# A fourth slab buffer for the slab behind a layer norm, and gate and up of a net's first step in one stream of 512-column matmuls

## The chip, the cores and the metric

One core of a Trainium2 chip runs the whole program. The time is the device time of one launch in microseconds (us). Before the change it is 1534.26 us, the median of 3 runs (1534.22 to 1534.91).

## The reference, cut to what matters

256 tokens of 1024 features pass through one block of a first kind and two layers of a second kind, all in f32:

```python
def first_block(...):          # once
    u = rmsnorm(h, norm_mix)
    # s5 branch and stick-breaking attention on u @ w_in, gated and merged
    h = h + merged @ w_out
    hid = relu(rmsnorm(h, norm_mlp) @ w_ff1)
    h = h + (hid * hid) @ w_ff2
    return rmsnorm(h, norm_final)

def swiglu(x, wg, wu, wd):
    return (silu(x @ wg) * (x @ wu)) @ wd

def second_block(...):         # l = 0, 1
    x = layer_norm(ALPHA*x + 0.5*swiglu(x, ffn1_wg[l], ffn1_wu[l], ffn1_wd[l]), ...)
    x = layer_norm(ALPHA*x + token_mixer(x, w_in[l], ..., w_out[l], ...), ...)
    x = layer_norm(ALPHA*x + 0.5*swiglu(x, ffn2_wg[l], ffn2_wu[l], ffn2_wd[l]), ...)
```

w_ff1 is 1024x4096, wg and wu are 1024x2816, wd is 2816x1024. There are thus five feed-forward nets: the plain one (relu squared) of the first block, called ffn1 below, and four gated ones, fa and fb of each layer l.

## The kernel before, in words

**Slabs.** Every weight is cut into slabs of 128 partitions x 2048 f32 (1 MB). A slab is loaded by SyncE (SP) into `raw` (`sp_slab`, the DMA is line 396), ScalarE (ACT) casts it to the rounded upper part `wh` (`act_round`, line 430), VectorE (DVE) subtracts to get the lower part `wl` (`dve_split`, line 437), and TensorE (PE) multiplies: each product is three matmuls, upper by upper, upper by lower, lower by upper (`mm3`, line 470; line 524 and 528 in the steps of a net, where one 512-column matmul covers upper and lower activations). `plan()` lays out one list of slabs and gives each one of three slots in turn. Four semaphores a slot order the work: SP waits for `split[slot]` before it overwrites `raw`, ACT waits for `raw_full[slot]` and for `used[slot]` of the slab before, DVE for `rounded[slot]`, PE for `split[slot]`.

**Order.** Each engine runs one order, written out by hand, and never goes past a wait. In a net `ffn_split` (lines 592 to 637) writes the same order for ACT and DVE: an opening, a loop over the steps, the last but one step, the last step. `do` is `act_round` or `dve_split` of a slab; `epilogue` is what evicts and combines the step's products. In ffn1 (16 steps of two slabs, 256 hidden features each) `step` runs first the epilogue and then `do` of the slab two places on. The numbers of slabs of ffn1 used below: 52, 54 are w_ff1 of steps 14 and 15, 53, 55, 56 are w_ff2 of steps 13, 14, 15, and 57, 58 are gate and up of the first step of net fa of layer 0. SP's order in ffn1 (`b1_sp`) is a loop that loads w_ff1 of step i and w_ff2 of step i-1, then the gains of the norm, then slab 56, then `b2_sp`: a table, and 57, 58.

**Between nets.** PE runs `rows_two` for the last two down slabs with the 128 tokens of tile 0 ahead of tile 1. For each tile DVE takes statistics (line 917) and writes the normed tile `res` (938, 947, or 944), PE transposes it (`turn_half`, line 883), ACT casts the upper part (893) and DVE subtracts the lower part (957). `big_act` rounds one slab in tile 0's part of the norm, and `big_dve` splits one slab (`next_split`) after tile 1's part.

**A gated net's start.** `first_tokens` multiplies the gate slab with the tokens as the stationary operand: tile 0 (24 matmuls of 256 columns), `turn_half` of tile 1, tile 1 (24 more). A second `first_tokens` does the up slab (48). Then step 1 begins: 8 matmuls of line 524, 8 of 528, four transposes of the first step's product (line 546), and so on. The same `first_tokens` opens the projection `in2` behind net fa, whose next slabs go through `lin_pe`.

**Other users of the buffers.** `late_prod` (8 KB a partition) is scratch of the first block's scan and of the attention; `bh`, `bl` hold split activations and the last step's hidden values.

Of the kernel before, what the change touches and what calls it, by code (L numbers as in the profile page):

```python
# [14 lines left out]
P = 128  # L15
# [15 lines left out]
WCOLS = SLAB // KD  # L31
PI = float(np.pi)
# [73 lines left out]
def plan():  # L106


    slabs, used, last = [], [0, 0, 0], [1, 2]

    def oldest():

        return 3 - sum(last)

    def add(what, part, slot=None):
        if slot is None:
            slot = oldest()
        slabs.append((what, part, slot, used[slot]))
        used[slot] += 1
        if slot != last[1]:  # L120
# [24 lines left out]
    g, s, d = oldest(), last[0], last[1]  # L145
    add("ff1", 0, g)
    for i in range(1, SLABS1):
        add("ff1", i, s)
        add("ff2", i - 1, d)
    add("ff2", SLABS1 - 1)  # L150

    def ffn(tag, l):
        g, d, u = oldest(), last[1], last[0]
        add(tag + "_g", (l, 0), g)
        add(tag + "_u", (l, 0), u)
        for i in range(1, SLABS2 - 1):
            add(tag + "_g", (l, i), g)
            add(tag + "_d", (l, i - 1), d)
            add(tag + "_u", (l, i), u)

        add(tag + "_g", (l, SLABS2 - 1), g)
        add(tag + "_u", (l, SLABS2 - 1), u)
        add(tag + "_d", (l, SLABS2 - 2), d)
        add(tag + "_d", (l, SLABS2 - 1))

    for l in range(LAYERS):
        mark(("fa", l))
        ffn("fa", l)
        mark(("in2", l))
        for n in (6, 0, 1, 2, 3, 4, 5):  # L170
            add("in2", (l, n))
        mark(("uq", l))
        add("uq", (l, 0))
        mark(("ukv", l))
        add("ukv", (l, 0))
        mark(("gate2", l))
        for n in range(8):
            add("gate2", (l, n))
        mark(("proj", l))
        for n, w in enumerate(("proj_m", "proj_n", "proj_m", "proj_n")):  # L180
            add(w, (l, n // 2))
        mark(("out2", l))
        for n in range(4):
            add("out2", (l, n))
        mark(("fb", l))
        ffn("fb", l)
    return slabs, where


def hybrid_ssm_attention_kernel(nc, a, out):  # L190
# [9 lines left out]
    loads_so_far, total = [], [0, 0, 0]  # L200
# [4 lines left out]
    with ExitStack() as ctx:  # L205
# [9 lines left out]
        raw = sb("raw", [P, 3, SLAB])  # L215
        wh = sb("wh", [P, 3, SLAB], F32R)
        wl = sb("wl", [P, 3, SLAB], F32R)
# [5 lines left out]
        bh = sb("bh", [P, KD, T], F32R)  # L223
        bl = sb("bl", [P, KD, T], F32R)
# [9 lines left out]
        late_prod = sb("late_prod", [P, 2, 4, T])  # L234
# [29 lines left out]
        raw_full = [sem(f"raw_full{i}") for i in range(3)]  # L264
        rounded = [sem(f"rounded{i}") for i in range(3)]
        split = [sem(f"split{i}") for i in range(3)]
        used = [sem(f"used{i}") for i in range(3)]
# [247 lines left out]
        def ffn_pe(pe, n0, iters, has_up, ih0, j):  # L515
# [70 lines left out]
            if has_up:  # L586
# [3 lines left out]
                     lambda: last_hidden(n1 + per, iters - 1, bh, bl))  # L590

        def ffn_split(eng, do, n0, iters, has_up, epilogue, opening, then=None):
# [29 lines left out]
            if last + 3 < len(slabs):  # L622
# [35 lines left out]
        def ffn_act_engine(act, n0, iters, has_up, ih0, j, scale):  # L658
            net = net_index(j)

            def epilogue(what, n, i, more, between=None):
# [23 lines left out]
                b = 6 if isinstance(i, int) and i == 1 and not has_up else 4  # L685
# [7 lines left out]
            def first_step(n, function, s):  # L693
                wait_used(act, n)
                act.activation(act_out[:, :, :], two(bank[4]), function).then_inc(s, 1)
# [5 lines left out]
            def opening_gated():  # L701
                act_round(act, n0 + 3)
                first_step(n0, ACT.Silu, ffn_act)
                act_round(act, n0 + 2)
                seed(act, j, 0, scale, 0)
                act_round(act, n0 + 4)
                round_product(7)
                epilogue("gate", n0 + 2, 1, 0)
                seed(act, j, 0, scale, 1)
                silu("gate", 1)  # L710
                act_round(act, n0 + 5)
                epilogue("up", n0 + 4, 1, 0)
                act_round(act, n0 + 6)

            def opening_plain():
                act_round(act, n0 + 2)
                first_step(n0, ACT.Relu, relu_done)
# [8 lines left out]
        def ffn_dve_engine(dve, n0, iters, has_up, ih0, j):  # L726
            net = net_index(j)

            def epilogue(what, n, i, more, between=None):

                if what == "gate" and not has_up and isinstance(i, int) and i == iters - 1:
                    link = lambda ins: chain(dve, dve_n, dve_chain, ins)
                    for f in range(2):
# [18 lines left out]
                        ins = dve.tensor_copy(bh[:, f, :], hid[:, f, :])  # L752
# [5 lines left out]
                        ins = dve.tensor_tensor(bl[:, f, :], hid[:, f, :], bh[:, f, :].bitcast(F32), ALU.subtract)  # L758
                    ins.then_inc(hid_ready, 1)
                    return  # L760
                if what == "gate":
                    dve.wait_ge(gate_half, i + (ih0 - net))
                    b = 6 if isinstance(i, int) and i == 1 and not has_up else 4
# [9 lines left out]
                if has_up and isinstance(i, int) and i == iters - 1:  # L773
# [5 lines left out]
                    link(dve.tensor_copy(bh[:, 0, :], hid[:, 0, :]))  # L779
                    dve.tensor_tensor(bl[:, 0, :], hid[:, 0, :], bh[:, 0, :].bitcast(F32), ALU.subtract)  # L780
# [24 lines left out]
                xh, xl = (bh[:, 0:2, :], bl[:, 0:2, :]) if last else (hh[:, :, :], hl[:, :, :])  # L805
# [265 lines left out]
        prod += [late_prod[:, i, :, :] for i in range(2)]  # L1071
# [42 lines left out]
        def first_tokens(pe, n, b, j=None):  # L1114
# [12 lines left out]
            mm.then_inc(used[slot], 1)  # L1127

# [51 lines left out]
        def b1_sp(sp):  # L1180
# [596 lines left out]
        def b1_act(act):  # L1777
# [121 lines left out]
            big_act(act, 2, N_FFN1 + 2 * SLABS1 + 1, 1)  # L1899

        def b1_dve(dve):
# [86 lines left out]
            big_dve(dve, 2, True, N_FFN1 + 2 * SLABS1 + 1)  # L1988
# [24 lines left out]
        late = late_prod[:, :, :, :].rearrange("p i a t -> p (i a t)")  # L2013
# [5 lines left out]
        cmp_w1 = [t_.rearrange("p (s c) -> p s c", s=16) for t_ in (late_prod[:, :, :, :].rearrange("p i a t -> p (i a t)"),  # L2019
# [33 lines left out]
        def b2_ffn_sp(sp, l, tag):  # L2053
            n0 = where[(tag, l)]
            sp_slab(sp, n0)
# [7 lines left out]
            gain_loads(sp, j)  # L2063
            for n in range(3 * SLABS2 - 4, 3 * SLABS2):
                sp_slab(sp, n0 + n)

        def b2_sp(sp, l):
# [4 lines left out]
            for n in range(where[("in2", l)], where[("fb", l)]):  # L2072
                if n == where[("in2", l)] + 4:
                    for i, nm in enumerate(("cmp_k_w1_2", "cmp_v_w1_2")):
# [276 lines left out]
        def b2_act(act, l):  # L2351
# [3 lines left out]
            big_act(act, nj, where[("in2", l)] + 1, 3)  # L2355
            n0 = where[("in2", l)]
            act_round(act, n0 + 2)
            wait_used(act, n0)
            act.copy(vsw, bank[5].rearrange("p (a w d) -> p a w d", a=NTT, w=2)).then_inc(v_read, 1)
            for i in range(6):  # L2360
                n = n0 + 1 + i
                act_round(act, n + 2)
# [83 lines left out]
            for q in range(3):  # L2446
                act_round(act, where[("out2", l)] + q + 2)
            big_act(act, nj + 1, where[("out2", l)] + 5, 3)
            ffn_act_engine(act, where[("fb", l)], SLABS2, True, SLABS1 + (2 * l + 1) * SLABS2, nj + 2, 2 * ALPHA)
            if l < LAYERS - 1:  # L2450
                big_act(act, nj + 2, where[("fb", l)] + 3 * SLABS2 + 1, 3)
# [42 lines left out]
        def b2_dve(dve, l):  # L2494
# [5 lines left out]
            big_dve(dve, nj, False, n0 + 1)  # L2500
            dve_split(dve, n0 + 2)
# [99 lines left out]
            for q in range(4):  # L2601
                if q < 3:
                    dve_split(dve, where[("out2", l)] + q + 2)
            big_dve(dve, nj + 1, False, where[("out2", l)] + 5)
            ffn_dve_engine(dve, where[("fb", l)], SLABS2, True, SLABS1 + (2 * l + 1) * SLABS2, nj + 2)
            if l < LAYERS - 1:
                big_dve(dve, nj + 2, False, where[("fb", l)] + 3 * SLABS2 + 1)
# [89 lines left out]
```

## Time and profile before

| | |
|---|---|
| profiled execution | 1534.03 us, of which the span is 1532.3 us |
| PE busy | 1504.0 us (98%), 9541 matmuls |
| DVE busy | 1059.5 us (69%) |
| ACT busy | 809.3 us (53%) |
| line 437, DVE (split) | x238, 513.7 us, mean 2170 ns |
| line 430, ACT (round) | x238, 429.0 us, mean 1812 ns |
| DMA | 265.08 MB, 173 GB/s |
| granted clock of TensorE | 0.999 |

PE is busy all but 28 us, so a step of another engine counts only where PE waits for it. A matmul's busy time (392 ns with 512 columns) is longer than the distance to the next one, since they are pipelined; distances are read from start to start.

### The profile page before, as it was taken

The numbers are of one execution on the slowest core, as the hardware profiler recorded it, in microseconds if no ns is written. First come the engines' busy times: TensorE is split into PE (matmuls) and PEld (weight loads), VectorE is DVE, ScalarE is ACT, GpSimd is POOL, SyncE is SP. The second block draws the span as 40 slices with busy tenths as digits, with TensorE's granted clock in tenths as the row PEclk, the third lists the DMA queues.
The fourth block names the chain that finished last, engine by engine and source line by source line (L and its number), as shares of the span: only waits on it lengthen the run. The fifth ranks groups of instructions, "written<-read, shape, count | busy, mean of one in ns | idle before, by whom it ended". The sixth has DMA issues, their size and how long they took to land.

```text
span 1532.3 us, 24066 instructions
## 1 busy us (share of the span) xinstructions
PE 1504.0 (98%) x9541; PEld 1321.5 (86%) x9541; DVE 1059.5 (69%) x1371; ACT 809.3 (53%) x1066; POOL 20.8 (1%) x50
## 2 busy tenths in 40 slices
PE   8999999999999999999999999999999999999998
PEld 7988988888888889898988888888889888888887
DVE  7999776667565666876766557665676866765666
ACT  7877653334444445666454444544445765454443
POOL 1011000000000000000000000000000000000000
PEclk9999999999999999999999999999999999999999
DMA  9432546556555666434455565465574524546653
GB/s 259 134 103 91 191 137 196 182 196 241 192 192 192 211 191 173 138 111 138 156 174 197 187 219 189 141 219 189 194 227 137 175 80 131 186 152 206 205 178 109
DMA packets 207021, 265.08 MB, mean 173 GB/s; under 512 B 14186, under 2 KB 176356, under 8 KB 206948
## 3 DMA queue, kind: packets, MB, share of 16 engines
q1 hardware_dynamic: 206884, 264.04, 53.6%
q8 instruction: 51, 0.84, 0.2%
q14 instruction: 22, 0.18, 0.0%
q10 hardware_dynamic: 64, 0.02, 0.0%
HBM read 262.99 MB, written 1.05 MB: 172 GB/s over the span
## 4 chain that ended last, share of the span: by engine, by line
PE 91%; DVE 6%; ACT 1%; DMA 0%; issue 0%; SPq 0%; DVEq 0%; ACTq 0%
PE bank L470 48%; PE bank L524 23%; PE bank L528 12%; DVE wl L437 2%; PE bank L2110 2%; PE bank L2124 1%; PE bank L1462 1%; PE bank L2139 1%; DVE u_parts L957 1%; ACT wh L430 1%; PE bank L1449 1%; DVE res L947 0%; DMA raw<-w_in 0%; DVE sq L938 0%; ACT u_parts L893 0%; PE bank L2114 0%
## 5 line engine op out<-in xcount | busy, mean ns | idle before, releaser
L437 DVE TENSOR_TENSOR wl<-raw,wh 128x2048 fp32r<-128x2048 f32 (+4 forms) x238 | 513.7, 2170 | 181.1 <-ACT wh L430 179.2
L430 ACT CAST wh<-raw 128x2048 fp32r<-128x2048 f32 (+4 forms) x238 | 429.0, 1812 | 121.8 <-PE bank L470 117.7
L524 PE MATMUL bank<-u_parts,wh 128*128 128x512 f32 x1520 | 380.0, 392 | 0.1
L524 PEld LDWEIGHTS bank<-u_parts,wh 128*128 128x128 f32 x1520 | 276.5, 189 | 52.3 <-issue 0.8
L470 PE MATMUL bank<-u_parts,wh 128*128 128x256 f32 (+1 forms) x1344 | 252.2, 289 | 7.0 <-DVE wl L437 4.5
L528 PEld LDWEIGHTS bank<-u_parts,wl 128*128 128x128 f32 x1520 | 207.4, 190 | 14.8
L470 PEld LDWEIGHTS bank<-u_parts,wh 128*128 128x128 f32 (+1 forms) x1344 | 208.1, 190 | 12.7 <-issue 7.0
L528 PE MATMUL bank<-u_parts,wl 128*128 128x256 f32 x1520 | 211.9, 282 | 0.0
L470 PE MATMUL bank<-u_parts,wl 128*128 128x256 f32 (+1 forms) x672 | 189.8, 282 | 0.0
L470 PE MATMUL bank<-wh,hh 128*128 128x512 f32 x440 | 172.3, 392 | 0.5
L470 PE MATMUL bank<-wl,hh 128*128 128x512 f32 x440 | 171.9, 391 | 0.0
L470 PE MATMUL bank<-wh,hl 128*128 128x512 f32 x440 | 171.3, 389 | 0.0
L470 PE MATMUL bank<-wh,u_parts 128*128 128x256 f32 (+1 forms) x608 | 139.1, 319 | 3.4 <-DVE u_parts L957 1.9
L470 PEld LDWEIGHTS bank<-u_parts,wl 128*128 128x128 f32 (+1 forms) x672 | 127.9, 190 | 0.0
L686 ACT COPY gates<-bank 128x512 f32<-128x512 f32 x54 | 31.6, 586 | 160.7 <-PE bank L528 160.7
L470 PEld LDWEIGHTS bank<-wh,u_parts 128*128 128x128 f32 x608 | 102.1, 190 | 13.9 <-DVE u_parts L957 3.4
L681 ACT COPY gates<-bank 128x512 f32<-128x512 f32 x36 | 21.1, 586 | 158.5 <-PE bank L528 158.5
L470 PEld LDWEIGHTS bank<-wh,hl 128*128 128x128 f32 x440 | 82.7, 188 | 17.6
L470 PEld LDWEIGHTS bank<-wh,hh 128*128 128x128 f32 x440 | 82.8, 188 | 16.8 <-issue 1.2
L470 PE MATMUL bank<-wl,u_parts 128*128 128x256 f32 (+1 forms) x304 | 96.3, 317 | 0.0
L470 PEld LDWEIGHTS bank<-wl,hh 128*128 128x128 f32 x440 | 82.8, 188 | 15.1
L792 DVE TENSOR_TENSOR gates<-gates,bank 128x512 f32<-128x512 f32 x36 | 24.8, 688 | 97.0 <-ACT gates L681 97.0
(371 smaller groups left out, 1780.7 us busy)
## 6 DMA issues: line engine op xcount, KB each, us to landing
raw<-ffn_wg SPq DMA_DIRECT2D x44, 1024.0 KB, 5.4
raw<-ffn_wu SPq DMA_DIRECT2D x44, 1024.0 KB, 5.3
raw<-ffn_wd SPq DMA_DIRECT2D x44, 1024.0 KB, 5.1
raw<-w_ff SPq DMA_DIRECT2D x32, 1024.0 KB, 5.3
raw<-w_in SPq DMA_DIRECT2D x28, 1024.0 KB, 6.1
raw<-w_out SPq DMA_DIRECT2D x12, 1024.0 KB, 4.9
raw<-w_gate SPq DMA_DIRECT2D x8, 1024.0 KB, 5.5
raw<-w_in SPq DMA_DIRECT2D x16, 512.0 KB, 5.3
```

The costliest lines, as they stand in the source:

```text
L430: ins = act.copy(dst, src)
L437: ins = dve.tensor_tensor(dst, src, upper.bitcast(F32), ALU.subtract)
L470: mm = pe.matmul(o, w, x, start=start and n == 0, stop=stop and n == 2, skip_group_check=True)
L524: return pe.matmul(two(bank[b + f]), slab_view(wh, slot, KD, WCOLS)[:, k, f * P:(f + 1) * P], u_parts[:, k, :, :], start=k == 0, stop=Fals ...
L528: return pe.matmul(bank[b + f][:, 0:T], slab_view(wl, slot, KD, WCOLS)[:, k, f * P:(f + 1) * P], uh[:, k, :], start=False, stop=k == KD - ...
L681: act.copy(up_z, halves(6)[1]).then_inc(up_half_out, 1)
L686: act.copy(gate_z, halves(b)[1]).then_inc(gate_half, 1)
L792: dve.tensor_tensor(up_z, up_z, halves(6)[0], ALU.add).then_inc(up_sum, 1)
L957: dve.tensor_tensor(ul[:, k, c], bank[2 * tt + half].rearrange("p (k t) -> p k t", k=4), uh[:, k, c].bitcast(F32), ALU.subtract).then_inc( ...
L1449: mm = pe.matmul(bank[s % 2][:, part * T:(part + 1) * T], b_t[part][r, i, :], us[r, i, :], start=True, stop=True, skip_group_check=True)
L1462: mm = pe.matmul(bank[3][32 * j:32 * j + 32, 0:T], c_t[c][:, s, :], prod[s % 4][:, q, :], start=n == 0, stop=n == 3)
L2110: pe.matmul(bank[e][:, c], q_(slice(tt * P, (tt + 1) * P)), k_(slice(0, (tt + 1) * P)), start=tt == 0, stop=True, skip_group_check=True)
```

## The change

A fourth slot, `LEAD` = 3, is added to `raw`, `wh`, `wl`. It takes the gate slab of each gated net's first step and the first slab of `in2`. To make room, `late_prod` becomes `raw[LEAD]`, and `bh`, `bl` become `wh[LEAD]`, `wl[LEAD]`; the last step's hidden values get small tiles `lasth`, `lastl`. The lead slab is rounded and split before the last but one step of the net ahead of it, and the slab behind it moves up by one place everywhere: what was split after the norm was the second slab, and is now the third.

```diff
-        bh = sb("bh", [P, KD, T], F32R)
-        bl = sb("bl", [P, KD, T], F32R)
+        bh, bl = (w[:, LEAD, :].rearrange("p (k t) -> p k t", k=KD) for w in (wh, wl))
+        lasth = sb("lasth", [P, 2, T], F32R)
+        lastl = sb("lastl", [P, 2, T], F32R)
...
@@ ffn_pe
-            first_tokens(pe, n0, 4, j - 1)
+            if has_up:
+                pair_tokens(pe, n0, 4, j - 1)
+            else:
+                first_tokens(pe, n0, 4, j - 1)
             n1 = n0 + (2 if has_up else 1)
-            if has_up:
-                first_tokens(pe, n0 + 1, 6)
-                pe.wait_ge(ffn_act, ih0 - SLABS1 + 1)
-                gate(n1, turn=7)
-            else:
+            if not has_up:
                 pe.wait_ge(res_copy_act, 4)
-                gate(n1, b=6, turn=5)
+            gate(n1, b=6, turn=4 if has_up else 5)
             down(n1 + 1, 0)
             if has_up:
+                pe.wait_ge(gate_sum, ih0 - net + 1)
                 up_half(n1 + 2, 0, 6)
...
@@ ffn_split (ACT and DVE)
             with eng.Fori(2, iters - 2, 1) as i:
                 turn(i, i - 1, n1)
+            last = n1 + per * (iters - 2)
+            lead = last + per + 1
+            if lead < len(slabs):
+                do(eng, lead)
             turn(iters - 2, 0, n1 + per * (iters - 3))
-            last = n1 + per * (iters - 2)
...
+            if has_up:
                 do(eng, last + 3)
+            else:
+                do(eng, lead + 1)
...
-                if last + 4 < len(slabs):
-                    do(eng, last + 4)
+                if lead + 1 < len(slabs):
+                    do(eng, lead + 1)
...
@@ opening_gated (ACT)
                 act_round(act, n0 + 3)
-                first_step(n0, ACT.Silu, ffn_act)
-                act_round(act, n0 + 2)
+                first_step(n0, halves(4)[1], ACT.Silu, ffn_act)
...
@@ opening_gated (DVE)
                 dve_split(dve, n0 + 3)
-                dve_split(dve, n0 + 2)
-                wait_used(dve, n0 + 1)
                 dve.wait_ge(ffn_act, ih0 - SLABS1 + 1)
-                dve.tensor_tensor(hid[:, :, :], act_out[:, :, :], two(bank[6]), ALU.mult).then_inc(hid_step, 1)
-                lower_product(7)
+                dve.tensor_tensor(hid[:, :, :], act_out[:, :, :], halves(4)[0], ALU.mult).then_inc(hid_step, 1)
+                lower_product(4)
...
+        def pair_tokens(pe, n, b, j):
+            slot = pe_slab(pe, n + 1)
+            pe_slab(pe, n)
+            both = lambda buf, k: buf[:, slot:LEAD + 1:LEAD - slot, k * WCOLS:(k + 1) * WCOLS]
+            for tt in range(NTT):
+                c = slice(tt * P, (tt + 1) * P)
+                if tt == 1:
+                    turn_half(pe, j, 1)
+                for k in range(KD):
+                    if k % 4 == 0:
+                        pe.wait_ge(norm_out, parts_count(j, tt, k // 4))
+                    if tt + 1 < NTT or k + 1 < KD:
+                        mm3(pe, two(bank[b + tt]), uh[:, k, c], ul[:, k, c], both(wh, k), both(wl, k), k == 0, k == KD - 1)
+                ... # tile 1, k = 7: six matmuls of 256 columns, so that each slot has its own release
...
@@ b1_sp
             with sp.Fori(1, SLABS1, 1) as i:
                 sp_slab(sp, n0 + 1, i, i - 1)
                 sp_slab(sp, n0 + 2, i - 1, i - 1)
+            sp.wait_ge(y_done, ST)
+            sp_slab(sp, where[("fa", 0)])
             sp.wait_ge(tok_out, out_count(BIG["mlp1"], 1, 1))
             gain_loads(sp, BIG["final1"])
...
@@ b2_ffn_sp
             gain_loads(sp, j)
+            if n0 + 3 * SLABS2 < len(slabs):
+                sp_slab(sp, n0 + 3 * SLABS2)
             for n in range(3 * SLABS2 - 4, 3 * SLABS2):
...
@@ b2_sp
+                if n == where[("out2", l)] + 1:
+                    sp.wait_ge(o_done, NU * (l + 1))
+                    sp_slab(sp, where[("fb", l)])
...
@@ ACT and DVE behind out2 (both alike)
-            for q in range(3):
-                act_round(act, where[("out2", l)] + q + 2)
-            big_act(act, nj + 1, where[("out2", l)] + 5, 3)
+            n = where[("out2", l)]
+            act_round(act, n + 2)
+            act_round(act, where[("fb", l)])
+            act_round(act, n + 3)
+            act_round(act, where[("fb", l)] + 1)
+            big_act(act, nj + 1, where[("fb", l)] + 2, 3)
```

## Rows read from the trace of the kernel before

**Rows 1.** The page's chain that ended last: share of the span by engine.

```profile
PE 91%; DVE 6%; ACT 1%; DMA 0%; issue 0%; SPq 0%; DVEq 0%; ACTq 0%
```

**Rows 2.** Busy time by stretch, two net openings: start:end, length, busy (count), clock, DMA.

```profile
769.50:784.20 14.70, 13.41 (x107) 12.58 (x106) 12.33 (x13) 7.96 (x9) 0.00 (x0) 1.00 0.24 76
389.80:403.50 13.70, 12.93 (x106) 12.48 (x106) 11.03 (x12) 7.96 (x9) 0.00 (x0) 1.00 0.27 83
```

**Rows 3.** Timeline of PE, opening of fa, layer 1: start, duration, line, [idle before].

```profile
962.20 0.66 PE L883 MATMUL bank<-ident,res 128*128 128x128 f32 x4 [0.80 <-DVE res L947]
...
966.45 0.39 PE L470 MATMUL bank<-wh,u_parts 128*128 128x256 f32 x1 [0.50 <-DVE wl L437]
```

**Rows 4.** Chain of waits in order of time: start, us; 512 columns, then 256.

```profile
354.34 5.47 PE bank L470 x24
...
611.53 5.75 PE bank L470 x48
```

**Rows 5.** Timeline of PE, opening of fa, layer 0.

```profile
392.75 1.23 PE L883 MATMUL bank<-ident,res 128*128 128x128 f32 x8
394.75 0.39 PE L470 MATMUL bank<-wh,u_parts 128*128 128x256 f32 x1 [0.77 <-DVE u_parts L957]
```

**Rows 6.** Timeline of PE, second slab of in2, layer 0.

```profile
585.76 0.50 PE L470 MATMUL bank<-u_parts,wh 128*128 128x256 f32 x2 [0.51 <-DVE wl L437]
```

**Rows 7.** Timeline of SP, end of ffn1: the loads' issues.

```profile
364.28 0.37 SPq L396 DMA_DIRECT2D raw<-w_ff  x1
364.86 0.35 SPq L985 DMA_DIRECT2D tmp<-norm_final  x1
```

**Rows 8.** Timeline of DVE, end of ffn1.

```profile
361.80 2.29 DVE L437 TENSOR_TENSOR wl<-raw,wh 128x2048 fp32r<-128x2048 f32 x1
366.02 0.69 DVE L764 TENSOR_TENSOR gates<-gates,bank 128x512 f32<-128x512 f32 x1 [1.94 <-ACT gates L686]
367.84 2.29 DVE L437 TENSOR_TENSOR wl<-raw,wh 128x2048 fp32r<-128x2048 f32 x1 [1.12 <-ACT wh L430]
```

**Rows 9.** Timeline of ACT, end of ffn1.

```profile
365.41 0.59 ACT L686 COPY gates<-bank 128x512 f32<-128x512 f32 x1 [3.64 <-PE bank L528]
365.89 1.92 ACT L430 CAST wh<-raw 128x2048 fp32r<-128x2048 f32 x1
...
373.69 0.37 ACT L674 COPY gates<-bank 128x256 f32<-128x256 f32 x1 [0.85 <-PE bank L528]
```

**Rows 10.** Timeline of PE, end of ffn1: last step's first matmul, last slab's first.

```profile
370.68 0.39 PE L524 MATMUL bank<-u_parts,wh 128*128 128x512 f32 x1
...
380.68 0.47 PE L470 MATMUL bank<-wh,bh 128*128 128x512 f32 x1 [1.53 <-DVE bl L758]
```

**Rows 11.** DMA issues at 542.92 and 543.35: count, KB, us to landing.

```profile
raw<-ffn_wu SPq DMA_DIRECT2D x1, 1024.0 KB, 5.3
...
raw<-ffn_wd SPq DMA_DIRECT2D x1, 1024.0 KB, 7.4
```

**Rows 12.** Timeline of PE, start of the program: matmuls on zeros.

```profile
4.86 3.57 PE L1004 MATMUL bank<-zero_w 128*128 128x256 f32 x15 [4.86 <-POOL cvalid L1230]
...
11.12 1.43 PE L1004 MATMUL bank<-zero_w 128*128 128x256 f32 x10
```

**Rows 13.** Busy time by stretch, end of the program; clock third from last.

```profile
1525.00:1526.00 1.00, 0.87 (x4) 0.38 (x2) 0.34 (x2) 0.00 (x0) 0.00 (x0) 1.00 1.01 375
1530.00:1531.00 1.00, 0.00 (x0) 0.00 (x0) 0.00 (x0) 0.00 (x0) 0.00 (x0) 0.85 1.00 375
```

**Rows 14.** Timelines of SP, ACT and DVE, end of fa, layer 0.

```profile
527.35 0.42 SPq L989 DMA_DIRECT2D tmp<-ln_f_b  x1
...
537.86 1.92 ACT L430 CAST wh<-raw 128x2048 fp32r<-128x2048 f32 x1
...
546.76 2.29 DVE L437 TENSOR_TENSOR wl<-raw,wh 128x2048 fp32r<-128x2048 f32 x1 [2.49 <-ACT wh L430]
```

**Rows 15.** Timeline of DVE, out2, layer 0: slabs 113 and 114.

```profile
752.22 4.65 DVE L437 TENSOR_TENSOR wl<-raw,wh 128x2048 fp32r<-128x2048 f32 x2 [1.11 <-ACT wh L430]
```

More of the change, by code:

```diff
@@ L31 @@
 WCOLS = SLAB // KD
+LEAD = 3
 PI = float(np.pi)
@@ L106, in plan @@
 def plan():
-    slabs, used, last = [], [0, 0, 0], [1, 2]
+    slabs, used, last = [], [0, 0, 0, 0], [1, 2]
     def oldest():
@@ L119, in add @@
         used[slot] += 1
-        if slot != last[1]:
+        if slot != LEAD and slot != last[1]:
             last[:] = [last[1], slot]
@@ L152, in ffn @@
     def ffn(tag, l):
-        g, d, u = oldest(), last[1], last[0]
-        add(tag + "_g", (l, 0), g)
+        g, d, u = last[0], last[1], oldest()
+        add(tag + "_g", (l, 0), LEAD)
         add(tag + "_u", (l, 0), u)
@@ L170, in plan @@
         for n in (6, 0, 1, 2, 3, 4, 5):
-            add("in2", (l, n))
+            add("in2", (l, n), LEAD if n == 6 else None)
         mark(("uq", l))
@@ L214, in hybrid_ssm_attention_kernel @@
         bank = [banks[:, i, :] for i in range(8)]
-        raw = sb("raw", [P, 3, SLAB])
-        wh = sb("wh", [P, 3, SLAB], F32R)
-        wl = sb("wl", [P, 3, SLAB], F32R)
+        raw = sb("raw", [P, 4, SLAB])
+        wh = sb("wh", [P, 4, SLAB], F32R)
+        wl = sb("wl", [P, 4, SLAB], F32R)
         res = sb("res", [P, KD, T])
@@ L261, in hybrid_ssm_attention_kernel @@
         affine = norm_small[:, 28:32].rearrange("p (a s) -> p a s", a=NTT)
[L264 to L267, printed above, removed]
+        raw_full = [sem(f"raw_full{i}") for i in range(4)]
+        rounded = [sem(f"rounded{i}") for i in range(4)]
+        split = [sem(f"split{i}") for i in range(4)]
+        used = [sem(f"used{i}") for i in range(4)]
         dve_chain, act_chain, pool_chain = sem("dve_chain"), sem("act_chain"), sem("pool_chain")
@@ L684, in epilogue @@
                     act.wait_ge(hid_ready, i + ih0)
-                b = 6 if isinstance(i, int) and i == 1 and not has_up else 4
+                b = 6 if isinstance(i, int) and i == 1 else 4
                 act.copy(gate_z, halves(b)[1]).then_inc(gate_half, 1)
@@ L691, in silu, with first_step @@
                     act.activation(act_out[:, :, :], gate_z, ACT.Silu).then_inc(ffn_act, 1)
-            def first_step(n, function, s):
+            def first_step(n, z, function, s):
                 wait_used(act, n)
-                act.activation(act_out[:, :, :], two(bank[4]), function).then_inc(s, 1)
+                act.activation(act_out[:, :, :], z, function).then_inc(s, 1)
             def round_product(b):
@@ L716, in opening_plain @@
                 act_round(act, n0 + 2)
-                first_step(n0, ACT.Relu, relu_done)
+                first_step(n0, two(bank[4]), ACT.Relu, relu_done)
                 for tt in range(NTT):
@@ L757, in epilogue @@
                             link(ins)
-                        ins = dve.tensor_tensor(bl[:, f, :], hid[:, f, :], bh[:, f, :].bitcast(F32), ALU.subtract)
+                        ins = dve.tensor_tensor(lastl[:, f, :], hid[:, f, :], lasth[:, f, :].bitcast(F32), ALU.subtract)
                     ins.then_inc(hid_ready, 1)
@@ L762, in epilogue @@
                     dve.wait_ge(gate_half, i + (ih0 - net))
-                    b = 6 if isinstance(i, int) and i == 1 and not has_up else 4
+                    b = 6 if isinstance(i, int) and i == 1 else 4
                     dve.tensor_tensor(gate_z, gate_z, halves(b)[0], ALU.add).then_inc(gate_sum, 1)
@@ L778, in epilogue @@
                     link(dve.tensor_tensor(hid[:, 0, :], act_out[:, 0, :], up_z[:, 0, :], ALU.mult))
-                    link(dve.tensor_copy(bh[:, 0, :], hid[:, 0, :]))
-                    dve.tensor_tensor(bl[:, 0, :], hid[:, 0, :], bh[:, 0, :].bitcast(F32), ALU.subtract)
+                    link(dve.tensor_copy(lasth[:, 0, :], hid[:, 0, :]))
+                    dve.tensor_tensor(lastl[:, 0, :], hid[:, 0, :], lasth[:, 0, :].bitcast(F32), ALU.subtract)
                     dve.wait_ge(up_half_out, i + (ih0 - SLABS1 + 1 - net))
@@ L804, in epilogue @@
                 last = isinstance(i, int) and i == iters - 1
-                xh, xl = (bh[:, 0:2, :], bl[:, 0:2, :]) if last else (hh[:, :, :], hl[:, :, :])
+                xh, xl = (lasth[:, :, :], lastl[:, :, :]) if last else (hh[:, :, :], hl[:, :, :])
                 dve.tensor_copy(xh, hid[:, :, :]).then_inc(hid_step, 1)
@@ L1070, in hybrid_ssm_attention_kernel @@
         prod = [small[:, i * 1024:(i + 1) * 1024].rearrange("p (a t) -> p a t", a=4) for i in range(2)]
-        prod += [late_prod[:, i, :, :] for i in range(2)]
+        prod += [raw[:, LEAD, i * 1024:(i + 1) * 1024].rearrange("p (a t) -> p a t", a=4) for i in range(2)]
         ATT = 3 * P
@@ L1127, in first_tokens @@
             mm.then_inc(used[slot], 1)
+        def pair_tokens(pe, n, b, j):
[11 more added lines that the diff above has]
+                        mm3(pe, two(bank[b + tt]), uh[:, k, c], ul[:, k, c], both(wh, k), both(wl, k), k == 0, k == KD - 1)
+                for x, w in ((uh, wl), (ul, wh), (uh, wh)) if tt == NTT - 1 else ():
+                    for i, s in enumerate((slot, LEAD)):
+                        mm = pe.matmul(two(bank[b + tt])[:, i, :], x[:, KD - 1, c], w[:, s, (KD - 1) * WCOLS:KD * WCOLS],
+                                       start=False, stop=True, skip_group_check=True)
+                        if x is uh and w is wh:
+                            mm.then_inc(used[s], 1)
         def lin_quarter(pe, n, b, j):
@@ L2012, in hybrid_ssm_attention_kernel @@
         ctok = [small[:, 512 + P * i:512 + P * (i + 1)] for i in range(2)]
-        late = late_prod[:, :, :, :].rearrange("p i a t -> p (i a t)")
+        late = raw[:, LEAD, :]
         probs = [flat(hid)[:, 0:ATT], flat(act_out)[:, 0:ATT], late[:, 0:ATT], late[:, ATT:2 * ATT]]
@@ L2018, in hybrid_ssm_attention_kernel @@
         x_f = [flat(t_).rearrange("p (s c) -> p s c", s=16) for t_ in (act_out, hid)]
-        cmp_w1 = [t_.rearrange("p (s c) -> p s c", s=16) for t_ in (late_prod[:, :, :, :].rearrange("p i a t -> p (i a t)"),
+        cmp_w1 = [t_.rearrange("p (s c) -> p s c", s=16) for t_ in (late,
                                                                     gflat[:, 2048:4096])]
@@ L2071, in b2_sp @@
             b2_ffn_sp(sp, l, "fa")
-            for n in range(where[("in2", l)], where[("fb", l)]):
+            for n in range(where[("in2", l)] + 1, where[("fb", l)]):
                 if n == where[("in2", l)] + 4:
+                    sp.wait_ge(split[LEAD], slabs[where[("in2", l)]][3] + 1)
                     for i, nm in enumerate(("cmp_k_w1_2", "cmp_v_w1_2")):
@@ L2354, in b2_act @@
             ffn_act_engine(act, where[("fa", l)], SLABS2, True, SLABS1 + 2 * l * SLABS2, nj, 2 * ALPHA)
-            big_act(act, nj, where[("in2", l)] + 1, 3)
+            big_act(act, nj, where[("in2", l)] + 2, 3)
             n0 = where[("in2", l)]
-            act_round(act, n0 + 2)
+            act_round(act, n0 + 3)
             wait_used(act, n0)
@@ L2600, in b2_dve @@
                 dve_up(dve, where[("proj", l)], l + 1, q)
[L2601 to L2604, printed above, removed]
+            n = where[("out2", l)]
+            dve_split(dve, n + 2)
+            dve_split(dve, where[("fb", l)])
+            dve_split(dve, n + 3)
+            dve_split(dve, where[("fb", l)] + 1)
+            big_dve(dve, nj + 1, False, where[("fb", l)] + 2)
             ffn_dve_engine(dve, where[("fb", l)], SLABS2, True, SLABS1 + (2 * l + 1) * SLABS2, nj + 2)
             if l < LAYERS - 1:
-                big_dve(dve, nj + 2, False, where[("fb", l)] + 3 * SLABS2 + 1)
+                big_dve(dve, nj + 2, False, where[("fb", l)] + 3 * SLABS2 + 2)
         J_LAST = 8
```

27 lines of the change are left out of this document (12 added, 15 removed).

## The prediction

> **What bounds the kernel now.** I read the chain of waits first. By engine, 91% of the span is TensorE and 6% VectorE [rows 1], so time is saved only where TensorE waits, or by making its stream shorter, and lost wherever something new makes it wait. The busy times by stretch say where it waits: the opening behind a norm. From the first product of tile 0 to the first matmul of step 1 it takes 14.6 us, in which TensorE is busy 13.4 [rows 2] (the first row, fb of layer 0; fa and fb of layer 1 have the same stretch to 0.1 us, so there are three openings of this kind). Behind ffn1 it takes 13.6 us (the second row there). The timeline of TensorE in that stretch names the waits: transposes that wait for DVE's normed tile, and the second slab, which waits 0.50 us for the split that stands behind the norm on DVE [rows 3]. The second slab of in2 waits 0.51 us for the same split [rows 6], once in each layer.
>
> **The opening, from 96 narrow products to a pair.** The chain of waits gives 24 matmuls of 512 columns 5.47 us, 228 ns each, and 48 of 256 columns 5.75 us, 119.8 ns each [rows 4]. The new opening is tile 0 of both slabs, 24 x 0.228 = 5.47; the eight transposes with the cast and the subtract behind them, 2.00 us from their start to the next product [rows 5] (392.75 to 394.75); tile 1, 21 x 0.228 + 6 x 0.120 = 5.51. Together 12.98. Tile 0 now lasts longer than DVE's work on tile 1: before, the last normed half let the transposes go at 962.20 [rows 3], 4.5 us after tile 0's first product at 957.7, against 5.47; so the wait for `res` is gone, and what is late next is the cast and subtract within the 2.00. Both slabs are split before the norm, so the wait of 0.50 is gone too. The gain is 14.6 - 13.0 = 1.6 us in three openings and 13.6 - 13.0 = 0.6 behind ffn1, 5.4 us in all. Of each, 45 x (2 x 119.8 - 228) ns = 0.5 us comes from wider matmuls, the rest from waits. The bounds: if the wide ones gave nothing and the transposes waited as before, the four gains would be near 2 us in all; the upper bound is the 2.00 shrunk by at most another 0.7 us each (the wait of 0.77 in it [rows 5]), 8 us.
>
> The Trainium skill has a formula that speaks against this part: "TensorE: Matmul & The Clock Gate", section "Back-to-back issue gap", gives the isolated distance as N/2.4 + 2.5 ns, so one wide matmul would save 2.5 ns against two narrow ones. By it the pairs would give 0.1 us a net and not 0.5, and the time below would be 1.6 us higher. The trace does not agree: 2 x 119.8 - 228 is 12 ns [rows 4].
>
> **What follows the pair.** Silu and the product with up now start when the pair ends. In the rows' durations that is some 1.5 us (one ACT and one DVE pass of 512 columns, 0.6 and 0.69, with their handovers), and the transposes of the product come 2.8 us after the pair: cost 0. Step 1's slab is split by then (DVE ends it some 2.3 us behind the norm, with 5.5 us of tile 1 to cover it). The added wait for `gate_sum` ahead of up stands behind a whole down slab, 5.47 us [rows 4], that hides a copy, a split and a sum (0.6 + 2.3 + 0.7): cost 0.
>
> **in2.** Its first slab is the lead, its second is split before the norm: the wait of 0.51 goes [rows 6], twice, 1.0 us. Bounds 0 and 1.0.
>
> **The lead's rounding and splitting in the nets fa and fb.** One more ACT pass of 1.9 and DVE pass of 2.3 us stand ahead of step 9. In fa of layer 0 ACT would do it at 537.86 [rows 14] and push the two works behind it; DVE has 2.49 us idle ahead of the next split [rows 14] (at 546.76), and that split is wanted by TensorE only at 554. The load is issued behind the gains, at some 527.8 [rows 14], and lands near 537.2 (about 3.1 MB ahead of and with it at some 370 GB/s, from 528): it is there 0.7 us before ACT asks. Cost 0; up to 1 us in each of three nets if it lands 3 us later. In out2 the split goes between slabs 113 and 114: DVE's two in a row start at 752.22 and take 4.65 us [rows 15]; with the lead between them slab 114 is ready at 759.1, and TensorE wants it at 760.8. Cost 0, in both layers.
>
> **The lead in ffn1: here the change adds a wait that nothing hides.** `ffn_split` puts the lead after step 13. SP's loop runs to the last step, so it issues slab 55 only when DVE has split 53, which is 361.80 + 2.29 [rows 8], the load goes out at 364.28 [rows 7], and the lead's load behind it at some 364.7. But ACT has rounded 53 by then, and its next instruction is the rounding of the lead. Two 1 MB loads issued 0.43 us apart landed 5.3 and 7.4 us after their issues [rows 11]; so the lead lands at 364.7 + 7.4 = 372.1. Behind the waiting ACT stand the eviction of step 14 (now at 365.41) and the rounding of 54 (365.89) [rows 9]; behind the waiting DVE the sum (0.69) and the split of 54 (2.29) [rows 8]. From there: ACT rounds the lead to 374.1, evicts and rounds 54 to 376.5; DVE splits the lead 374.2 to 376.4, sums to 377.0, splits 54 to 379.3. TensorE wanted 54 at 370.68 [rows 10]. It has nothing else in its order, and is still for 8.6 us. The bounds are 6.5 (the lead landing 5.3 us after its issue, as a lone load does) and 9.6 (the gains and slab 56 sharing the engines with it).
>
> The later part of ffn1 moves with it: from 370.68 to the last slab's first product it was 10.0 us, of which 1.53 waiting [rows 10], set by DVE from the eviction at 373.69 [rows 9] on; that chain had 0.9 us of slack ahead, since DVE was splitting.
>
> **The clock after such a stop.** At the end of the program TensorE is idle from 1525.9, the granted clock is 1.00 at first and falls within 1530 to 1531 [rows 13], 4 to 5 us later. A stop of 8.6 us is longer, so it will fall from 2.4 to 1.2 GHz. At the program's start 15 matmuls of 256 columns took 3.57 us and ten later ones 1.43 [rows 12], so coming back costs 3.57 - 15 x 0.12 = 1.8 us of work. It lies in front of the eviction that sets the chain; less the slack of 0.9 it is 0.9 us. If the first half of the step (2.8 us of work) all ran at half the clock, it is 1.9. I take 1.2; the lower bound is -0.1, no fall.
>
> The Trainium skill has this as a rule, in "TensorE: Matmul & The Clock Gate", Part 1: an idle array goes to half its clock and returns only after sustained work. By that rule, the trace agrees [rows 12, 13]; without it the sum would be 1.3 us lower, the first rival below.
>
> **The sum.** 1534.03 (the profiled execution; its span 1532.3 and 1.7 around it) + 8.6 + 1.2 - 5.4 - 1.0 = 1537.4. The median of the runs lies 0.2 above that execution; I say 1537.5. The rest of the change (scratch moved into slot 3, small tiles) moves no instruction.
>
> **The rivals.** 0.2% is 3.1 us, about what a measurement of this kernel tells from no change: 1531.2 to 1537.3 is "same".
>
> *The clock holds* (or returns at once): 1536.2. For it: the end of the program is the one place where the trace shows it falling. Against it: the stop is twice as long as what it took there. Not slower. It decides from 0.3 us of the 1.2 on, so it is near the forecast.
>
> *The wait in ffn1 is hidden*, with all the gains left: 1534.3 - 6.4 = 1527.9. The point from which it decides: each us that the lead lands earlier is one us less; to be faster by 0.2% it must land near 366.8 or before. Against it, the issue at 364.28 of the load ahead of it [rows 7] and 5.3 us for even a lone load.
>
> *The openings give little*: TensorE reads two slots' halves in one matmul slower than one row of them, or the transposes, now behind the whole pair of tile 0, are what tile 1 waits for, or a lead in fa or fb lands late. Gains of 2 in place of 6.4: 1542.
>
> **How the numbers follow.** The forecast (stall, fallen clock, gains as counted) 0.47, with its own range 1536.5 to 1539.5; clock holds 0.27; openings give little 0.13; stall hidden or short 0.13. Slower by over 0.2%: two thirds of the forecast's cases, the openings' case and a few of the second, 0.50; same 0.37; faster 0.13. The range 1533.8 to 1541.5 leaves out the hidden stall and half of the openings' case.
>
> **What would show it.** A gap of TensorE of 8 to 9 us ahead of ffn1's last step, with ACT's rounding of `ffn_wg` waiting some 10 us for a DMA before it, and the granted clock at half behind it. Openings of 13.0 us with matmuls of 512 columns 228 ns apart. No wait at in2's second slab, and no new gap between steps 8 and 10 of fa and fb or in out2. I am wrong if the gap is not there: then the lead's load went out before slab 55's, or ACT was not behind it.

## The result and the profile after

The changed kernel takes 1537.64 us, median of 12 runs (1537.15 to 1538.39); the kernel before, on the same chip, 1534.25 (12 runs, 1533.90 to 1534.91). The ratio is 1.0023, 95% interval 1.0015 to 1.0031: slower by 3.4 us, and the 1537.64 is 0.14 above the forecast of 1537.5. The profiled execution of after took 1537.29 with a span of 1535.5.

The shares of the chain by engine, the row that answers to [rows 1]:

```profile
PE 93%; DVE 5%; ACT 1%; DMA 1%; issue 0%; SPq 0%; DVEq 0%; ACTq 0%
```

TensorE has gone from 91 to 93% and VectorE from 6 to 5%: the waits behind the norms are shorter. DMA's share, rounded, is 1% where it was 0: the chain of both kernels has one load at the program's start (7.41 us before, 6.26 after), and that of after has a second one of 7.38 us, at the end of ffn1. The issues on SP there, against [rows 7]; then ACT, DVE and TensorE, against [rows 8, 9, 10] (start, duration, engine, line, operation, count, and the idle time before it with what ended it):

```profile
359.25 5.38 SPq L397 DMA_DIRECT2D raw<-w_ff  x2
364.84 0.38 SPq L397 DMA_DIRECT2D raw<-ffn_wg  x1
```

```profile
359.82 1.92 ACT L431 CAST wh<-raw 128x2048 fp32r<-128x2048 f32 x1 [3.07 <-PE bank L471]
372.25 1.90 ACT L431 CAST wh<-raw 128x2048 fp32r<-128x2048 f32 x1 [10.51 <-DMA raw<-ffn_wg]
374.05 0.58 ACT L692 COPY gates<-bank 128x512 f32<-128x512 f32 x1
374.53 3.70 ACT L431 CAST wh<-raw 128x2048 fp32r<-128x2048 f32 x2
384.39 0.37 ACT L680 COPY gates<-bank 128x256 f32<-128x256 f32 x1 [6.16 <-PE bank L529]
```

```profile
374.18 2.29 DVE L438 TENSOR_TENSOR wl<-raw,wh 128x2048 fp32r<-128x2048 f32 x1 [10.11 <-ACT wh L431]
376.39 0.68 DVE L769 TENSOR_TENSOR gates<-gates,bank 128x512 f32<-128x512 f32 x1
376.99 2.28 DVE L438 TENSOR_TENSOR wl<-raw,wh 128x2048 fp32r<-128x2048 f32 x1
380.98 2.28 DVE L438 TENSOR_TENSOR wl<-raw,wh 128x2048 fp32r<-128x2048 f32 x1
```

```profile
379.42 3.75 PE L525 MATMUL bank<-u_parts,wh 128*128 128x512 f32 x8 [8.61 <-DVE wl L438]
...
384.13 1.99 PE L525 MATMUL bank<-u_parts,wh 128*128 128x512 f32 x8
...
390.62 0.47 PE L471 MATMUL bank<-wh,lasth 128*128 128x512 f32 x1 [0.80 <-DVE lastl L763]
```

Read them from the top. SP issues the load of the lead (`ffn_wg`) at 364.84, behind slab 55's. ACT has been waiting for it since 361.74 and rounds it at 372.25. The copy for step 14, which it did at 365.41 before [rows 9], stands behind that and runs at 374.05; then come two roundings in a row, of slabs 54 and 55. DVE waits 10.11 us for the lead, splits it, sums, and splits slab 54 by 379.27. TensorE stands still for 8.61 us ahead of the last step. The idle time that the costliest group of TensorE's lines gives as ended by a split is this one stop:

```profile
L525 PE MATMUL bank<-u_parts,wh 128*128 128x512 f32 x1520 | 381.8, 394 | 8.7 <-DVE wl L438 8.6
```

The granted clock around it, in windows of 1 us (start:end, length, busy and count of PE, PEld, DVE, ACT and POOL, then the clock, the DMA share and GB/s):

```profile
372.00:373.00 1.00, 0.00 (x0) 0.00 (x0) 0.00 (x0) 0.75 (x1) 0.00 (x0) 1.00 1.01 401
373.00:374.00 1.00, 0.00 (x0) 0.00 (x0) 0.00 (x0) 1.00 (x1) 0.00 (x0) 0.60 1.04 418
374.00:375.00 1.00, 0.00 (x0) 0.00 (x0) 0.82 (x1) 1.00 (x3) 0.00 (x0) 0.50 1.01 406
...
382.00:383.00 1.00, 1.00 (x4) 0.71 (x4) 1.00 (x1) 0.00 (x0) 0.00 (x0) 0.50 1.08 385
383.00:384.00 1.00, 1.00 (x8) 1.00 (x7) 0.26 (x1) 0.00 (x0) 0.00 (x0) 0.78 0.87 301
384.00:385.00 1.00, 1.00 (x7) 0.87 (x6) 0.21 (x1) 0.61 (x2) 0.00 (x0) 1.00 0.26 54
```

It falls to half (1.2 GHz) early between 373 and 374, some 2.4 us into the stop (TensorE is idle from 370.81), and comes back in the middle between 383 and 384, some 4 us after TensorE resumed at 379.42. The eight matmuls of 512 columns at 379.42 take 3.75 us, the next eight of the same kind, at 384.13, take 1.99.

An opening, fa of layer 1, against [rows 2, 3] (timeline of TensorE):

```profile
964.77 0.39 PE L471 MATMUL bank<-wh,u_parts 128*128 128x512 f32 x1
...
970.22 1.04 PE L886 MATMUL bank<-ident,res 128*128 128x128 f32 x8
972.22 0.51 PE L471 MATMUL bank<-wh,u_parts 128*128 128x512 f32 x1 [0.96 <-DVE u_parts L960]
972.56 0.40 PE L471 MATMUL bank<-wl,u_parts 128*128 128x512 f32 x1
...
977.87 1.32 PE L525 MATMUL bank<-u_parts,wh 128*128 128x512 f32 x5
```

Tile 0 takes 5.45 us, the eight transposes run at once (no idle time ahead of them), the next product is 2.00 behind their start, tile 1 takes 5.65. Together 13.10. And the second slab of in2, layer 0, against [rows 6]: its first matmul is 0.12 us behind the last of the first slab, with no wait.

```profile
594.27 0.28 PE L471 MATMUL bank<-wh,u_parts 128*128 128x256 f32 x1
594.39 0.40 PE L471 MATMUL bank<-u_parts,wh 128*128 128x256 f32 x2
594.63 0.28 PE L471 MATMUL bank<-u_parts,wl 128*128 128x256 f32 x1
```

I laid the two traces beside each other at matching matmuls: after is 9.94 us late at ffn1's last slab (390.62 against 380.68 [rows 10]). From there it gains 0.57 in fa's opening of layer 0, 0.81 in in2, 1.50 in fb's, then 1.51, 0.84 and 1.50 in layer 1: 6.73 in all, and the end is 3.21 late. Between these places the offset stays within 0.03 us, so nothing else in fa, fb or out2 moved the end. All this is the profiled execution. The cost of the stop is not the same in every run: seven of the twelve took 1537.15 to 1537.72 us with a mean clock of 0.996 to 0.997, five took 1538.06 to 1538.39 with 0.995 to 0.996.

### The profile page after: what moved, and what is told of

Same layout as the page of the kernel before. It is cut to its first block, busy times and chain, and to the rows that moved or that the text cites. A ratio compares the mean times of both kernels' runs of the same rounds, so it can differ in the third digit from the quotient of the medians.

```text
span 1535.5 us, 23711 instructions
## 1 busy us (share of the span) xinstructions
PE 1500.9 (98%) x9361; PEld 1313.3 (86%) x9361; DVE 1058.2 (69%) x1371; ACT 807.8 (53%) x1066; POOL 20.7 (1%) x50
## 4 chain that ended last, share of the span: by engine, by line
PE 93%; DVE 5%; ACT 1%; DMA 1%; issue 0%; SPq 0%; DVEq 0%; ACTq 0%
PE bank L471 49%; PE bank L525 23%; PE bank L529 12%; PE bank L2141 2%; DVE wl L438 1%; PE bank L2155 1%; PE bank L1488 1%; PE bank L2170 1%; ACT wh L431 1%; PE bank L1475 1%; DMA raw<-ffn_wg 0%; DVE u_parts L960 0%; PE bank L2145 0%; PE bank L886 0%; DMA small<-log_dt 0%; PE bank L2131 0%
## 5 line engine op out<-in xcount | busy, mean ns | idle before, releaser
L471 PE MATMUL bank<-wh,u_parts 128*128 128x512 f32 (+1 forms) x472 | 129.3, 356 | 5.0 <-DVE u_parts L960 5.0
L471 PEld LDWEIGHTS bank<-wh,u_parts 128*128 128x128 f32 x472 | 84.1, 189 | 19.4 <-DVE u_parts L960 6.6
L471 PE MATMUL bank<-wl,u_parts 128*128 128x512 f32 (+1 forms) x236 | 83.5, 354 | 0.0
```

The lines of the kernel that those rows point to most:

```text
L471: mm = pe.matmul(o, w, x, start=start and n == 0, stop=stop and n == 2, skip_group_check=True)
```

## The experiments

Is it the place of the lead's load that costs, and is it the whole of the loss? In e1_early_load SP issues it one step earlier, ahead of the last step's two slabs, and the rest stays:

```diff
-            with sp.Fori(1, SLABS1, 1) as i:
+            with sp.Fori(1, SLABS1 - 1, 1) as i:
                 sp_slab(sp, n0 + 1, i, i - 1)
                 sp_slab(sp, n0 + 2, i - 1, i - 1)
             sp.wait_ge(y_done, ST)
             sp_slab(sp, where[("fa", 0)])
+            sp_slab(sp, n0 + 2 * SLABS1 - 3)
+            sp_slab(sp, n0 + 2 * SLABS1 - 2)
```

> The changed kernel with one thing moved: SP issues the lead's load of ffn1 ahead of the loads of the last step's slabs, one step (11 us) earlier; ACT's and DVE's order is unchanged. My theory (ACT and DVE waited for that load, and TensorE for them): the gap of 8.6 us ahead of ffn1's last step and the half clock behind it are gone, TensorE's first product of the last slab comes 10.0 us after the last step's first matmul as before, and all gains stay: 1537.6 - 9.9 = 1527.7 us. Rival 1, the extra rounding and splitting itself delays TensorE in ffn1: a gap of some 2.3 us stays there, 1530. Rival 2, the fallen clock was the main cost: 1536.4.

Measured 1527.68 us (5 runs, 1527.57 to 1527.72), ratio to before 0.9957 (0.9944 to 0.9971). The load now goes out at 353.83 and lands 7.6 us later, some 0.3 us before ACT asks for it. Its timeline and TensorE's:

```profile
359.85 3.73 ACT L431 CAST wh<-raw 128x2048 fp32r<-128x2048 f32 x2 [3.07 <-PE bank L471]
365.41 0.59 ACT L692 COPY gates<-bank 128x512 f32<-128x512 f32 x1 [1.83 <-PE bank L529]
```

```profile
370.67 1.98 PE L525 MATMUL bank<-u_parts,wh 128*128 128x512 f32 x8
...
380.68 0.47 PE L471 MATMUL bank<-wh,lasth 128*128 128x512 f32 x1 [1.53 <-DVE lastl L763]
```

The lead's rounding (the second of the two at 359.85) fits where ACT idled, the copy is at 365.41 as before, and the last step and the last slab stand where they stood [rows 10]. So the stop and its clock cost the 9.9 us between 1537.64 and 1527.68 (each against its own runs of before), and the openings with in2 are worth 6.5. Both rivals fall: no gap of 2.3 us is left, and far more than the clock's part has come back.

Does the position in ACT's and DVE's order cost, or the position of the load? In e2_round_later the load stays late, and the plain net rounds and splits the lead one step later:

```diff
-            if lead < len(slabs):
+            if has_up and lead < len(slabs):
                 do(eng, lead)
             turn(iters - 2, 0, n1 + per * (iters - 3))
+            if not has_up:
+                do(eng, lead)
```

> The changed kernel with ffn1's lead rounded and split behind the last but one step instead of ahead of it; its load is where it was. My theory: the load has landed by then (372.1), the gap ahead of the last step is gone, but the split (2.3 us) now stands ahead of DVE's chain for the last slab, which TensorE awaits: 1527.7 + 2.2 = 1529.9 us. Rival (only the place of the load counts, whoever waits for it): 1537.6.

Measured 1531.28 (11 runs, 1529.66 to 1532.55), ratio 0.9982 (0.9973 to 0.9991): 1.4 above what was expected. The stop of 8.6 us is gone, but a smaller one stands ahead of the last slab, and in it the clock falls (timeline, then windows):

```profile
383.06 0.76 PE L471 MATMUL bank<-wh,lasth 128*128 128x512 f32 x1 [3.74 <-DVE lastl L765]
```

```profile
382.00:383.00 1.00, 0.00 (x0) 0.00 (x0) 0.89 (x4) 1.00 (x2) 0.00 (x0) 0.81 1.10 347
383.00:384.00 1.00, 0.94 (x2) 0.83 (x3) 1.00 (x1) 0.02 (x1) 0.00 (x0) 0.50 1.06 340
385.00:386.00 1.00, 1.00 (x4) 0.81 (x3) 0.24 (x1) 0.00 (x0) 0.00 (x0) 0.50 0.96 385
386.00:387.00 1.00, 1.00 (x5) 0.82 (x5) 0.70 (x1) 0.00 (x0) 0.00 (x0) 0.98 0.59 71
```

Three microseconds at half are 1.5 us of work, and the last slab is 2.2 us later than in the kernel with the early load (383.06 against 380.68, less 0.17, by which this execution is already late at the ACT rounding: 360.02 against 359.85). 1527.7 + 2.2 + 1.5 = 1531.4. The expectation had the wait and not the clock. The runs bear that out: one of the eleven took 1529.66 with a mean clock of 0.999, close to the 1529.9 expected without a fall; seven took 1531.12 to 1531.41 with 0.998, and three 1532.08 to 1532.55 with 0.997. So behind the same stop a run lost nothing, some 1.6 or some 2.6 us, and its mean clock goes along; only one of those with 0.998 has a trace. Either edit takes the long stop away; only the earlier load takes all of it.

How much does the clock cost? In e5_keep_clock sixty matmuls on zeros into a free bank keep TensorE busy in the stop:

```diff
             n1 += per * (iters - 2)
+            if not has_up:
+                keep_clock(pe, 60, 6)
             gate(n1, 0, iters - 1, by_tile=not has_up)
```

> The changed kernel with 60 matmuls of 256 columns on zeros into an unused bank ahead of ffn1's last step (7.2 us of work, inside the gap of 8.6). My theory of the clock's part: the granted clock stays at 2.4 GHz, and the last slab's first product follows the last step's first matmul by 9.9 us, not 11.2: 1537.6 - 1.3 = 1536.3 us. Rival (the 1.2 us came from the order of splits, not from the clock): 1537.6.

Measured 1535.77 (11 runs, 1535.60 to 1536.13), ratio 1.0011 (1.0002 to 1.0020). Timeline of TensorE, to be held against the two rows of after:

```profile
370.69 7.35 PE L1009 MATMUL bank<-zero_w 128*128 128x256 f32 x60
379.60 2.08 PE L525 MATMUL bank<-u_parts,wh 128*128 128x512 f32 x8 [1.56 <-DVE wl L438]
```

The wait for the data ends at nearly the same time (379.60 for 379.42), but the eight matmuls take 2.08 us, not 3.75, and the clock stays at 1.00. From the step's first matmul to the last slab's it is 9.36 us here (to 388.96) and 11.20 in after. The clock costs 1.84 us in this pair of executions, and the medians, 1.87 apart, say the same. Expected were 1.3: the rival (the order of splits, not the clock) falls, and the price was taken 0.5 too small.

How much do the 512-column matmuls give, and how much the order? Two kernels with the early load. In the first, e3_narrow, each wide matmul is two of 256 columns, and the order stays:

```diff
-                        mm3(pe, two(bank[b + tt]), uh[:, k, c], ul[:, k, c], both(wh, k), both(wl, k), k == 0, k == KD - 1)
+                    for i, s in enumerate((slot, LEAD)) if tt + 1 < NTT or k + 1 < KD else ():
+                        q = slice(k * WCOLS, (k + 1) * WCOLS)
+                        mm3(pe, two(bank[b + tt])[:, i, :], uh[:, k, c], ul[:, k, c], wh[:, s, q], wl[:, s, q],
+                            k + i == 0, k == KD - 1)
```

> e1_early_load with the pair's matmuls cut into two of 256 columns in the same order (96 in place of 51 matmuls a net). What the wide ones are worth by the rows of before, 45 x 12 ns in each of four nets: 2.1 us, so 1529.8 us. Rival, 2.5 ns each: 1528.2. If the two-slot operand made the wide ones slower than one row of 512, it would be under 1527.7.

Measured 1529.55 (6 runs, 1529.34 to 1529.70), ratio 0.9969 (0.9957 to 0.9981): 1.87 us above the wide one, over 4 openings of 45 wide matmuls each, so 10.4 ns for each. That is near the forecast's 12 [rows 4]. From the isolated distance, N/2.4 + 2.5 ns, in the Trainium skill's "TensorE: Matmul & The Clock Gate", section "Back-to-back issue gap", the estimate is 2.5 ns for each, 0.45 us in all; the two medians differ by four times that.

In the second, e4_slab_order, the slabs come one after the other, as before the change, and only the early split is left:

```diff
-            for tt in range(NTT):
-                c = slice(tt * P, (tt + 1) * P)
-                if tt == 1:
-                    turn_half(pe, j, 1)
+            for i, s in ((1, LEAD), (0, slot)):
+                for tt in range(NTT):
+                    c = slice(tt * P, (tt + 1) * P)
+                    if tt == 1 and i == 1:
+                        turn_half(pe, j, 1)
...
-                first_step(n0, halves(4)[1], ACT.Silu, ffn_act)
+                first_step(n0 + 1, halves(4)[1], ACT.Silu, ffn_act)
```

> e3_narrow (1529.55 us) with the order of the opening turned back: the lead slab's two tiles first, then the second slab's two tiles, 96 matmuls of 256 columns; the slabs are still both split ahead of the norm, and silu waits for the second slab. So the transposes of tile 1 wait for DVE's normed tile again. My theory: tile 1 begins 5.06 us after tile 0 as in the kernel before, then 72 x 0.12 us follow, 13.8 against 13.5 us, in three openings +0.3, behind ffn1 +0.1: 1530.6 us. Rival: the new order is what the openings gained from, then it is near the old 14.6 us, 1532.5.

Measured 1530.28 (9 runs, 1530.06 to 1531.01), ratio 0.9975 (0.9965 to 0.9985). The transposes of tile 1 in the opening of fa, layer 1, and the product behind them:

```profile
959.85 0.66 PE L886 MATMUL bank<-ident,res 128*128 128x128 f32 x4
961.29 0.66 PE L886 MATMUL bank<-ident,res 128*128 128x128 f32 x4 [0.79 <-DVE res L950]
961.90 0.39 PE L471 MATMUL bank<-wh,u_parts 128*128 128x256 f32 x1
```

The wait for `res` [rows 3] is back, but from the first transpose to the product it is 2.05 us, and in after, where the wait is gone, 2.00: there the product waits 0.96 for the cast and subtract instead. So the pair's order is worth little, 1530.28 - 1529.55 = 0.73 us, 0.18 an opening. The 3.8 us that this kernel is ahead of its own runs of before (1534.12) belong to the early splits: 1.65 in in2 (the two offsets above) and some 2.2 in the openings. The trace agrees: this opening takes 13.83 us (956.82 to 970.65) and took 14.57 (957.74 to 972.31), 0.74 less, and there are three of its kind.

The openings still hold the 0.96 us ahead of tile 1 and the transposes themselves. The last kernel, e6_early_turn, with the early load and the wide pair, puts the transposes of tile 1 into tile 0's stream, the first half ahead of block 6 and the second at its end:

```diff
-                if tt == 1:
-                    turn_half(pe, j, 1)
                 for k in range(KD):
...
+                    if tt == 0 and k == 6:
+                        turn_part(pe, j, 1, 0)
...
+                if tt == 0:
+                    turn_part(pe, j, 1, 1)
```

> e1_early_load (1527.68 us) with tile 1's transposes moved into tile 0's matmuls: half 0 after the sixth k, half 1 at the end of tile 0, in the four gated openings. In the changed kernel TensorE has an idle 1.1 of the 2.0 us from the transposes to tile 1's first product. My theory: the normed half is there 3 us after tile 0's start, the transposes at 4.1 us make tile 1 ready at 6.1, and tile 0 with its transposes ends at 6.4, so the idle goes in all four: 1527.7 - 4.4 = 1523.3 us. Rival: the normed halves are late, or what follows the pair (silu, product, transposes) becomes the wait: 1525 to 1527.7.

Measured 1522.85 (5 runs, 1522.75 to 1523.07), ratio 0.9926 (0.9913 to 0.9940). It is faster than both kernels. The same opening, by its end and in one window from its first product to step 1:

```profile
956.85 0.60 PE L891 MATMUL bank<-ident,res 128*128 128x128 f32 x4
...
958.68 0.60 PE L891 MATMUL bank<-ident,res 128*128 128x128 f32 x4
959.03 0.48 PE L471 MATMUL bank<-wh,u_parts 128*128 128x512 f32 x1
```

```profile
952.74:964.62 11.88, 11.88 (x61) 9.95 (x60) 9.61 (x12) 4.56 (x5) 0.00 (x0) 1.00 0.03 8
```

TensorE is busy in all of the 11.88 us; with the early load alone the stretch was 13.09 (954.98 to 968.07). Four times 1.2 is the 4.8 between 1527.68 and 1522.85. The transposes come in two groups of four with the last six matmuls of tile 0 between them, so the first cast and subtract have those to cover them, and the second have the first four blocks of tile 1.

## Why the prediction was right, step by step

**The stop in ffn1: right in place, cause and size.** 8.6 us were predicted, and 8.61 of idle time measured (8.7 from the step's old start to its new one: 370.68 to 379.42). Every link of the chain came within 0.2 us: landing 372.1 and measured 372.2; the lead rounded at 374.1 and 374.15; split of 54 ending at 379.3 and 379.27. The choice of 7.4 us from issue to landing [rows 11], not the 5.3 of a lone load, made it: the load took 7.38 here. The early load took the stop away and put the end at 1527.68, where the forecast had 1527.9 for a hidden wait.

**The clock: right that it falls; the sum met by luck, with two errors of opposite sign.** 1.2 us were taken for the clock after the slack; the kernel with zeros shows 1.84 on the chain, of some 2.0 us of work lost in 4 us at half. The slack of 0.9 was not where it was put: it is in the warm chain, which got shorter by 0.64 us (9.36 against 10.00), where I had 0.1. The cause is in ACT's rows: 54 and 55 were rounded in one go at 374.53, so DVE no longer waited for the rounding of 55 and split it 1.56 us behind the step's first matmul (380.98 - 379.42, and the same in the kernel with zeros); before it was 2.20 (372.88 - 370.68). In both warm kernels DVE's sum for the step's first eviction stands directly behind that split (375.09 and 383.37), so the 0.64 between the two is what the chain got shorter. So the sum 1.84 - 0.64 = 1.2 met the 1.2 taken by luck, by two terms each 0.5 to 0.6 off. The first rival (the clock holds) fell. The Trainium skill says in "TensorE: Matmul & The Clock Gate", Part 1, that an idle array goes to half its clock and comes back only after sustained work; the windows of after agree (0.50 at 374, after 3.2 us idle, and 1.00 again some 4 us behind the first matmul).

**The openings: right.** 13.10 us for 12.98 predicted in fa of layer 1; the remainder is tile 1, 5.65 for 5.51, whose first matmul behind the wait is 0.34 us ahead of the second (972.22 to 972.56) where 0.228 was counted. The gains were 0.57, 1.50, 1.51 and 1.50, together 5.1 for 5.4. What was late next was the cast and subtract, as said, at 2.00. What the step did not say is that the wait for `res`, which went, gave almost nothing, since the cast and subtract took its place; the gain is the split's wait (0.74 in the kernel with slabs one after the other) and the wider matmuls (1.87 over four openings, 0.47 each); with the 0.18 of the order that is 1.4 of the 1.5. Of the rival (the openings give little) nothing is left: a matmul that reads two slots' halves has the distance of 0.23 of one that reads a row.

**in2: the mechanism right, the term too small.** 0.5 a layer was counted from the idle column [rows 6], and 0.81 and 0.84 were gained. That column runs from a matmul's modelled end, 0.28 us behind its start, while starts without a wait are 0.12 apart. 0.16 is missing from each wait that is read that way, so 0.51 was 0.67. Another 0.10 is the first matmul behind the wait: in before the third stands 0.34 us behind it (585.76 to 586.10, below), in after 0.24 (594.39 to 594.63). The last 0.04 to 0.07 is open.

```profile
586.10 0.28 PE L470 MATMUL bank<-u_parts,wl 128*128 128x256 f32 x1
```

**The edits costed at nothing: right.** The offset does not move between the openings, so the leads in fa and fb, the split in out2 and the wait for `gate_sum` were hidden. The lead in fa of layer 0 was nearer to a wait than the 0.7 us said (and 3.1 MB at 370 GB/s from 528 is 536.4, not the 537.2 written): in the kernel with narrow matmuls ACT waits 0.26 us for that load (`w_in`), which TensorE does not feel.

```profile
538.33 3.72 ACT L431 CAST wh<-raw 128x2048 fp32r<-128x2048 f32 x2 [0.26 <-DMA raw<-w_in]
```

**The sum.** 8.7 + 1.84 - 0.64 - 6.73 = +3.2, by the spans 1535.5 - 1532.3 = 3.2, for +3.4 forecast (8.6 + 1.2 - 6.4). The misses in the gains, 0.3 less than forecast in the openings and 0.65 more in in2, have opposite signs too, and both are smaller than the spread of the runs.

## What to carry to other kernels

When an instruction is moved forward in the order of an engine that works in order, move the load that feeds it forward in its queue too, and look up when it lands; everything written behind it waits with it, even what is ready. Here a change that gave 6.5 us cost 9.9 by the place of one load. Add to a stop of TensorE what the clock costs behind it (here 1.5 to 1.8 us in the traces, and it varied from run to run), and price a wait between short matmuls by the distance of the starts, not by the idle column.

## What the runs showed of the hardware

In the stop of 3.74 us the clock already fell (0.81 in the last microsecond of it, 0.50 in the next), and one run of that kernel in eleven, with a mean clock of 0.999, had the time expected without a fall. In the stop of 8.61 us it fell some 2.4 us in; at the end of the program before it was 4 to 5 us. After the stop of 8.61 us half clock lasted some 4 us more, and after that of 3.74 until some 386, 3 us. Sixty matmuls on zeros, 7.35 us, and then 1.56 us idle kept the eight behind them at full speed. One matmul of 512 columns that reads halves of two slots took 10.4 ns less than two of 256.
